# Values and half of the keys of the gated delta heads turned to tokens by 32x32 transpositions and a way through DRAM

## The reference

```python
rhs = jnp.concatenate([vc * bc[..., None], kc * (bc * jnp.exp(gam))[..., None]], axis=-1)
sol = lax.linalg.triangular_solve(lhs, rhs, left_side=True, lower=True, unit_diagonal=True)
...
k_end = kc * jnp.exp(gam[..., -1:] - gam)[..., None]
...
u = wv - jnp.einsum('bhtd,bhde->bhte', wk, S)
o = jnp.einsum('bhtd,bhde->bhte', qd, S) + jnp.einsum('bhts,bhse->bhte', qk_c, u)
S_new = ge[..., None, None] * S + jnp.einsum('bhsd,bhse->bhde', ke, u)
```

## Time and profile before

| | us |
|---|---|
| median of 3 runs | 2143.75 |
| lowest, highest | 2143.62, 2144.07 |
| the profiled execution, its own time | 2146.69 |
| its span, first to last instruction | 2145.0 |
| mean granted TensorE clock | 0.997 of full |

### The profile page before, as it was taken

How to read it: one execution, slowest core, us unless ns; L and a number is a source line. 1 busy time by engine, 2 the same in 40 slices (tenths; PEclk the granted TensorE clock), 3 DMA queues, 4 the chain that set the end, 5 groups by cost and what they waited for, 6 DMA issues and landing times.

```text
span 2145.0 us, 30741 instructions
## 1 busy us (share of the span) xinstructions
PE 2126.3 (99%) x11364; PEld 1757.1 (82%) x11364; DVE 1298.0 (61%) x1625; ACT 1109.0 (52%) x1472; POOL 165.5 (8%) x265
## 2 busy tenths in 40 slices
PE   9999999999999999999999999999999999999998
PEld 7888888888888787888878888878888788888886
DVE  6446555464544867676766564566546845566466
ACT  6554545454444848474755454445444544545443
POOL 7000000000000100101010000100001211000012
PEclk9999999999999999999999999999999999999999
DMA  9856566666565555454646755755558566555654
GB/s 338 266 182 212 174 217 191 196 199 222 179 205 177 154 163 155 145 165 134 180 145 210 259 185 177 213 151 173 187 190 293 181 210 180 177 164 179 203 176 159
DMA packets 211577, 410.98 MB, mean 192 GB/s; under 512 B 14096, under 2 KB 31009, under 8 KB 211070
## 3 DMA queue, kind: packets, MB, share of 16 engines
q1 hardware_dynamic: 199440, 369.94, 55.2%
q0 software_dynamic: 9712, 30.98, 4.7%
q10 hardware_dynamic: 2304, 8.39, 1.1%
HBM read 395.19 MB, written 14.07 MB: 191 GB/s over the span
## 4 chain that ended last, share of the span: by engine, by line
PE 90%; DVE 4%; ACT 3%; issue 3%; DMA 1%; DVEq 0%; ACTq 0%; SPq 0%
PE stream_psum L669 27%; PE stream_psum L671 26%; PE stream_psum L670 26%; PE heads_psum L639 2%; ACT w_high L1108 1%; DVE w_low L1538 1%; DVE work L1724 1%; ACT work L1108 1%; PE heads_psum L1025 1%; PE heads_psum L988 1%; PE heads_psum L969 1%; PE heads_psum L860 1%; PE heads_psum L841 1%; DMA w_raw<-in_w_mem_kv 1%; PE heads_psum L790 0%
## 5 line engine op out<-in xcount | busy, mean ns | idle before, releaser
L1538 DVE TENSOR_TENSOR w_low<-w_raw,w_high 128x1024 fp32r<-128x1024 f32 x688 | 829.8, 1224 | 624.4 <-ACT w_high L1108 622.6
L1108 ACT ACTIVATE w_high<-w_raw 128x1024 fp32r<-128x1024 f32 x688 | 711.8, 1057 | 463.7 <-PE stream_psum L671 365.3
L669 PE MATMUL stream_psum<-w_high,x_high 128*128 128x512 f32 x1856 | 739.5, 398 | 1.6 <-issue 1.6
L671 PE MATMUL stream_psum<-w_high,x_low 128*128 128x512 f32 x1856 | 723.8, 390 | 0.0
L670 PE MATMUL stream_psum<-w_low,x_high 128*128 128x512 f32 x1856 | 723.0, 390 | 0.0
L669 PEld LDWEIGHTS stream_psum<-w_high,x_high 128*128 128x128 f32 x1856 | 348.7, 188 | 74.6 <-issue 4.0
L671 PEld LDWEIGHTS stream_psum<-w_high,x_low 128*128 128x128 f32 x1856 | 348.4, 188 | 73.8
L670 PEld LDWEIGHTS stream_psum<-w_low,x_high 128*128 128x128 f32 x1856 | 348.8, 188 | 70.0 <-issue 1.9
L669 PE MATMUL stream_psum<-w_high,y_high 128*128 128x512 f32 x896 | 353.2, 394 | 2.1 <-DVE y_low L2001 2.1
L671 PE MATMUL stream_psum<-w_high,y_low 128*128 128x512 f32 x896 | 349.5, 390 | 0.0
L670 PE MATMUL stream_psum<-w_low,y_high 128*128 128x512 f32 x896 | 349.4, 390 | 0.0
(11 more groups left out here) (324 smaller groups left out, 1272.2 us busy)
## 6 DMA issues: line engine op xcount, KB each, us to landing
w_raw<-in_w_in SPq DMA_DIRECT2D x528, 512.0 KB, 4.4
w_raw<-in_w_out SPq DMA_DIRECT2D x128, 512.0 KB, 5.1
w_raw<-in_w_mem_kv SPq DMA_DIRECT2D x32, 512.0 KB, 5.8
turned_scratch<-work POOLq DMA_DIRECT2D x40, 128.0 KB, 3.5
work<-turned_scratch POOLq DMA_DIRECT2D x10, 512.0 KB, 5.6
work<-rows_scratch POOLq DMA_DIRECT2D x8, 512.0 KB, 5.1
proj<-in_mem_t SPq DMA_DIRECT2D x8, 256.0 KB, 7.1
work<-in_x_t SPq DMA_DIRECT2D x4, 512.0 KB, 7.0
```

The source lines that it names most:

```text
L669: pe.matmul(acc, hi[:, k, sl(m)], w, start=first, stop=False)
L671: return pe.matmul(acc, lo[:, k, sl(m)], w, start=False, stop=final)
L1108: return act.activation(dst, src, func, **kw)
L1538: tt(WL[:, c % RING, :], RAW[:, c % RING, :], WH[:, c % RING, :].bitcast(F32), ALU.subtract).then_inc(lo_done, 1)
```

## The change

Keys (their first 128 tokens, the only ones that the state update reads) and values no longer pass TensorE. VectorE transposes their 32x32 blocks in SBUF (`turned_k`, `turned_v`), which leaves each block inside its own 32 partitions. GpSimd stores the result in DRAM with eight DMAs, four of 128 KB (values) and four of 64 KB (keys), and loads it back with two, in an order that puts tokens on the partitions. Values then lie in four pieces of 32 features per row of partitions, and the products with them read and write through views of four pieces. VectorE scales both in SBUF (`ke`, `v`) just before `tt6`. The key products `kk` take the place in the step list where `k0t` stood; the steps of VectorE behind `nq` stand one step earlier.

```diff
@@ -90,7 +90,8 @@
     rel_d = nc.dram_tensor("rel_scratch", (A_H, COPIES, BIASW), F32, kind="Internal").ap()
-    turned_d = nc.dram_tensor("turned_scratch", (P, U), F32, kind="Internal").ap()
+    turned_d, values_d = [nc.dram_tensor(f"turned_{n}scratch", (P, U), F32, kind="Internal").ap() for n in ("", "values_")]
+    keys_d = nc.dram_tensor("turned_keys_scratch", (P, NBLK), F32, kind="Internal").ap()
     memt_d = [nc.dram_tensor(f"mem_{n}_scratch", (P, KT, S), F32, kind="Internal").ap() for n in ("high", "low")]
@@ -165,6 +166,7 @@
         turned_out, turned_in = sem("turned_stored"), sem("turned_loaded")
+        values_out, values_in = sem("turned_values_stored"), sem("turned_values_loaded")
         rows_out, rows_in, kv_in = sem("rows_stored"), sem("rows_loaded"), sem("kv_loaded")
@@ -182,7 +184,7 @@
         EIGHT = range(1, 7)
-        DN_PE = steps_of(sem("dn_pe"), ["k", "q", "v", "ssk", "k0t", "kk0", "kk1", "ssq", "vt0", "vt1", "qk0", "qk1"]
+        DN_PE = steps_of(sem("dn_pe"), ["k", "q", "v", "ssk", "kk0", "kk1", "ssq", "qk0", "qk1"]
                       + [f"{n}{l}" for l in LVS for n in ("x", "t")] + ["x6", "tt6"]
@@ -194,9 +196,9 @@
         DN_V = steps_of(sem("dn_dve"), ["g"] + conv_names(1) + conv_names(0) + ["silu1"] + conv_names(2)
-                        + ["nk", "silu0", "silu2", "ke", "at0", "at1", "at2", "at3", "at51", "at53", "at6", "nq", "v0", "v1"]
+                        + ["nk", "turned_k", "silu0", "silu2", "turned_v", "at0", "at1", "at2", "at3", "at51", "at53", "at6", "nq"]
                         + [f"row{k}" for k in EIGHT] + [f"{n}{k}" for k in EIGHT for n in ("part", "less")]
-                        + ["inv8", "tt2", "t2", "qkt0", "qkt1", "t3", "tt3", "t4", "full1", "full3", "top0", "top1", "full2", "full23", "t5", "full01", "full0", "tt6"]
+                        + ["inv8", "tt2", "t2", "qkt0", "qkt1", "t3", "tt3", "t4", "full1", "full3", "top0", "top1", "full2", "full23", "t5", "full01", "full0", "ke", "v", "tt6"]
                         + ["f1a", "r0", "r1", "r2", "r3", "f1b", "ss", "rs", "fr", "fg"])
@@ -556,6 +558,14 @@
                     if l == 4:
+                        wait_alone(pool, *done(DN_V, "turned_v", g))
+                        for a in range(4):
+                            for d, u, n in ((values_d, 11, S), (keys_d, 10, P)):
+                                pool.dma_start(bass.AP(d.tensor, a * n, [[4 * n, QUART], [QUART * 4 * n, 4], [1, n]]),
+                                               wk(u, 4 * n)[sl(a, QUART), :].rearrange("p (c r) -> p c r", c=4)).then_inc(values_out, 16)
+                        wait_alone(pool, values_out, g * 128 + 128)
+                        pool.dma_start(wk(2), values_d).then_inc(values_in, 16)
+                        pool.dma_start(wk(10, NBLK), keys_d).then_inc(values_in, 16)
                         pool.wait_ge(*done(DN_PE, "x3", g))
@@ -803,7 +813,8 @@
                 AT, TTs = wk(5).rearrange("p (s t) -> p s t", t=P), wk(7).rearrange("p (s t) -> p s t", t=P)
-                V = wk(2).rearrange("p (h m t) -> p h m t", h=4, m=M)
+                V = wk(2).rearrange("p (c h m t) -> p h m c t", c=4, h=4, m=M)
+                by_parts = lambda ap: ap.rearrange("p (c t) -> p c t", c=4)
                 KE = wk(11, 512).rearrange("p (h t) -> p h t", h=4)
@@ -826,11 +837,6 @@
                 yield from gap(6)
-                pe.wait_ge(*done(DN_V, "nk", g))
-                for h in range(4):
-                    last = tr(H[:, 2, sl(h)], CV[:, 1, h, 0:P])
-                last.then_inc(*signal(DN_PE, "k0t"))
-                yield from gap(2)

@@ -861,25 +867,16 @@

-                pe.wait_ge(*done(DN_V, "conv233", g))
+                pe.wait_ge(*done(DN_V, "nk", g))
                 products("kk", 0, 1)
-                yield
+                yield from gap(3)
                 pe.wait_ge(*done(DN_ACT, "sqq", g))
-                pe.wait_ge(*done(DN_V, "ke", g))
                 for i in range(2):
...
                 yield from gap(2)
-                pe.wait_ge(*done(DN_V, "silu2", g))
-                pe.wait_ge(*done(DN_ACT, "lnq", g))
-                for p in range(2):
-                    for h in (0, 1):
-                        for m in range(M):
-                            last = tr(H[:, 2 + p, sl(2 * h + m)], CV[:, 2, 2 * p + h, sl(m)])
-                    last.then_inc(*signal(DN_PE, f"vt{p}"))
-                yield from gap(2)
-                yield from gap(2)
-                pe.wait_ge(*done(DN_V, "v1", g))
+                yield from gap(4)
+                pe.wait_ge(*done(DN_V, "nq", g))
                 products("qk", 2, 0)
@@ -910,7 +907,7 @@
                 for h in range(4):
-                    last = pe.matmul(H[:, 0, sl(h)], TT[:, h, 0, :], V[:, h, 0, :], start=True, stop=True)
+                    last = pe.matmul(by_parts(H[:, 0, sl(h)]), TT[:, h, 0, :], V[:, h, 0], start=True, stop=True)
                 last.then_inc(*signal(DN_PE, "u0"))
@@ -929,7 +926,7 @@
                 for h in range(4):
-                    last = pe.matmul(H[:, 1, sl(h)], TT[:, h, 1, :], V[:, h, 1, :], start=True, stop=True)
+                    last = pe.matmul(by_parts(H[:, 1, sl(h)]), TT[:, h, 1, :], V[:, h, 1], start=True, stop=True)
                 last.then_inc(*signal(DN_PE, "u1"))
@@ -1735,17 +1732,21 @@
                 tt(wk(1), wk(1), wk(7), ALU.mult).then_inc(*signal(DN_V, "nk"))
+                dve.wait_ge(*done(DN_V, "nk", g))
+                dve.transpose(wk(10, NBLK).rearrange("p (c h t) -> p h c t", c=4, h=4), CV[:, 1, :, 0:P].rearrange("p h (c t) -> p h c t", c=4)).then_inc(*signal(DN_V, "turned_k"))
                 yield
...
                 stt(wk(2), wk(8), 1.0, wk(2), ALU.add, ALU.mult).then_inc(*signal(DN_V, "silu2"))
-                yield from gap(2)
-                dve.wait_ge(*done(DN_PE, "k0t", g))
-                tt(wk(11, 512).rearrange("p (s t) -> p s t", t=P), bank(2).rearrange("p (s t) -> p s t", t=P),
-                   cols(KD[:, bass.ds(g * 4, 4)], P), ALU.mult).then_inc(*signal(DN_V, "ke"))
-                yield from gap(2)
+                yield
+                dve.wait_ge(*done(DN_V, "silu2", g))
+                for i in range(2):
+                    last = dve.transpose(wk(11).rearrange("p (c i s t) -> p i s c t", c=4, i=2, s=4)[:, i],
+                                         wk(2 + i / 2, 512).rearrange("p (s c t) -> p s c t", s=4, c=4))
+                last.then_inc(*signal(DN_V, "turned_v"))
+                yield from gap(3)

@@ -1772,12 +1773,6 @@
                 yield
-                for p in range(2):
-                    dve.wait_ge(*done(DN_PE, f"vt{p}", g))
-                    tt(wk(2 + p / 2, 512).rearrange("p (s t) -> p s t", t=P), bank(2 + p).rearrange("p (s t) -> p s t", t=P),
-                       cols(HB[:, bass.ds(g * 4 + 2 * p, 2), :].rearrange("p h m -> p (h m)"), P), ALU.mult).then_inc(*signal(DN_V, f"v{p}"))
-                yield
-
                 wait_alone(dve, *done(DN_PL, "u8", g))
@@ -1841,18 +1836,25 @@
                 transposed(0)
-                yield from gap(2)
+                yield
+                dve.wait_ge(values_in, g * 32 + 32)
+                by_heads = lambda ap, n: ap.rearrange("p (c s t) -> p c s t", c=4, s=n)
+                tt(wk(11, NBLK).rearrange("p (s c t) -> p c s t", s=4, c=4), by_heads(wk(10, NBLK), 4),
+                   cols(over(KD[:, bass.ds(g * 4, 4)], 4), QUART), ALU.mult).then_inc(*signal(DN_V, "ke"))
+                tt(by_heads(wk(2), 8), by_heads(wk(2), 8),
+                   cols(over(HB[:, bass.ds(g * 4, 4), :].rearrange("p h m -> p (h m)"), 4), QUART), ALU.mult).then_inc(*signal(DN_V, "v"))
+                yield
                 dve.wait_ge(*done(DN_PE, "tt6", g))
...
                 F1 = wk(10.5, 512).rearrange("p (s t) -> p s t", t=P)
-                V = wk(2).rearrange("p (h m t) -> p h m t", h=4, m=M)
+                V = wk(2).rearrange("p (c h m t) -> p h m c t", c=4, h=4, m=M)
                 dve.wait_ge(*done(DN_PE, "qs", g))
...
                 for h in range(4):
-                    stt(V[:, h, 1, :], H[:, 2, sl(h)], NEB[:, bass.ds(g * 4 + h, 1), 1], V[:, h, 1, :], ALU.mult, ALU.add).then_inc(*signal(DN_V, f"r{h}"))
+                    stt(V[:, h, 1], H[:, 2, sl(h)].rearrange("p (c t) -> p c t", c=4), NEB[:, bass.ds(g * 4 + h, 1), 1], V[:, h, 1], ALU.mult, ALU.add).then_inc(*signal(DN_V, f"r{h}"))
                 yield from gap(2)
```

## The result

The changed kernel takes 2155.18 us (median of 5 runs, 2153.21 to 2156.44) against 2144.07 for the kernel before, run beside it: ratio 1.0044 (95% interval 1.0033 to 1.0056). That is slower by more than the 0.2% I called noise, and outside my range. The profiled execution took 2155.14 us with a span of 2153.0, 8.0 us longer than before's 2145.0.

A forecast was written before the change was run, and what follows sets the result against it. TensorE, busy in 99% of the span, was taken as the bound. Per group 1.38 us saved less waits of 0.9 and 0.45 left 0.3 to 0.5 us in all: 2143.4 us forecast, range 2140.8 to 2147.6.

The forecast's parts named there:

- GpSimd and DMA: Eight stores and two loads on GpSimd in the delta stage: hidden, priced at nothing, bounds 0 and 2 us per group.
- TensorE's saving: Twelve key and value transposes leave TensorE in each group: 1.38 us per group saved, 5.5 in all.
- First new wait: At chunk 256, `turned_k` delays the query silu, ScalarE and `w_low`: TensorE waits 0.9 us per group.
- Second new wait: At the group's end the norm comes before `w_low` of chunk 269: TensorE waits 0.45 us per group.
- Chunks 258 and 259: Behind chunk 256, with inversion steps moved up: slack of 0.2 us at 258 and 0.7 at 259, so no wait.
- `ke` and `v`: VectorE's scalings before `tt6`, 0.6 and 1.1 us: priced at nothing; uncovered they would cost 1.8 us per group.
- `ut4`: GpSimd's product that TensorE's `x4` needs: ready in time behind the ten issues, with room for 2.1 to 2.5 us.
- (c): Rival: GpSimd's issues and stores make `ut4` late for TensorE's `x4`; 3.2 us a group, 2156 us, or 2148.5; chance 0.12.
- (a): Rival: only one of the two new waits comes, giving back 1.8 to 3.6 us: 2140 to 2142 us; chance 0.15.
- (b): Rival: TensorE's full saving of 5.5 us, `w_low` of 256 on time: 2138.2 us, or 2137.0; chance 0.06.
- (d): Rival: small losses (thin slacks, update in pieces, late weight loads) of 0.5 to 1 us a group: 2145.4 to 2147.4 us; chance 0.17.

The follow-up runs named there:

- e8: The changed kernel again, unedited, for a second profile and time: 2153.78 us, ratio 1.0035 to the kernel before.
- e7: The changed kernel with its eight stores but without the two loads and VectorE's wait for them: 2146.50 us, ratio 1.0005 to the kernel before.
- after: The changed kernel as first measured and profiled, against the kernel before: 2155.18 us, ratio 1.0044.
- e1: The changed kernel without the ten DMAs and VectorE's wait for them: 2146.37 us, ratio 1.0005 to the kernel before.
- e6: The changed kernel with the order of e4 and the DMAs moved early, loads right behind `ut3`: 2141.82 us, ratio 0.9981 to the kernel before.
- e4: The changed kernel with `turned_k` behind the query silu and the norm one slot later: 2149.03 us, ratio 1.0017 to the kernel before.
- e5: The changed kernel with the order of e4 and without the ten DMAs: 2142.78 us, ratio 0.9986 to the kernel before.
- e2: The changed kernel with TensorE's 12 transposes a group put back, results unused: 2156.83 us, ratio 1.0053 to the kernel before.
- e9: The changed kernel with the early DMAs of e6 but VectorE's order unchanged: 2146.40 us, ratio 1.0009 to the kernel before.

## Why the prediction was wrong

**The step that failed** is in "GpSimd and DMA": "The added 6 MB over the stage are small against 411 MB; a weight load a microsecond later meets a ring with several microseconds to spare. Price nothing, bounds 0 and 2 us per group." I asked which data the new transfers could delay, found only weights, and compared bytes over the whole run. The stream that had no spare microseconds was TensorE's own instructions, and my own showed it: I read the start of `x4` there and not its 1.11 us. The runs price the loads at 7.3 us (e8 against e7), and 7.0 by the chunks of e8's trace, 5.3 by those of after's: 1.3 to 1.8 us a group, inside the bounds that I wrote beside the zero and then left out of the range. The Trainium skill, page "Runtime: NRT & Kernel Launch", section "Instruction fetch mechanics", says that instructions come in blocks of 16 KiB by a DMA queue of their own and that the cost is mostly hidden. On the size the trace agrees (1.36 MB in 83 packets); hidden it is not in the small products beside 768 KB of loads, where TensorE runs 64 products in 0.75 us, against some 0.23 us for one stream matmul.

**TensorE's saving**: 1.38 a group forecast, 1.3 measured (5.2 in all, not 5.5). Right in kind, a little too large. My sign for it, 5 us less busy time, failed in after (1.3 less), where TensorE also ran a stretch at the lower clock; in e1 it is 5.2 less and in e6 6.3.

**First new wait**: 0.9 forecast, 0.88 measured, 0.65 in group 3 (forecast 0.15 less there; it was 0.23). The cause was right: e4 and e5 move `turned_k` behind the query silu and the wait is gone; e2 gives TensorE its old work back and the wait is gone too. **Second new wait**: 0.45 forecast, 0.47, 0.46, 0.50 and 0.38 measured. Chunks 258 and 259 do not wait, `ke` and `v` are hidden (VectorE doesn't wait for the load), and `ut4` waited for x3 and not the other way round. What I left out is the 0.15 us that the chunk behind the second wait loses. With loads out of the way the chain as forecast remains, and e1, e7 and e9 lie 0.8, 0.9 and 1.9 us above the kernel before, where I had it 0.3 to 0.5 below. By the chunks of their traces 0.3 to 0.6 of that is in the stage (the smaller saving and the 0.15 a group); the rest is outside it and has no cause here.

**The rivals.** (c) had the right sign and the right suspect, the eight stores and two loads, but the wrong way: it went through `ut4`, which was in time, and e7 shows the stores free. That its 2156 lies near the measured time is chance. (a) and (b) fail, since both waits came. (d) named weight loads late beside the traffic. They were: from 690 to 1200 us ScalarE waits ten times and 23.7 us in all for `w_raw`, against five times and 9.3 before. But of these waits none reached TensorE. So the slower side had a chance of 0.11 from one mechanism, and the mechanism that decided was not on the list.

**What stays open.** The timed difference to before is 11.1 us in the first set and 8.2 in the second, of which the account has the loads' 7 and 0.5 to 1.9 for the rest; the first set holds some 2 us that I can't place, and its profile shows 2.0 ahead of the stage that e8's doesn't. Stops that end at the lower clock may be more frequent in the timed runs than in the profiled ones; a time alone does not show it. Why a packet of instructions starts later while loads are in flight (its place in a queue, or a DMA engine that is taken) wasn't tried, nor why it was late enough for small stops in e5, without any load. And 2.7 us of e2's median have no cause here.

## What to carry to other kernels

Before pricing a transfer at nothing, look at which stretch of the compute engine it lands in: beside big matmuls (e6, e9) 768 KB stopped TensorE nowhere, beside bursts of small ones 1.3 to 1.8 us a group, where the fetch of the engine's own instructions had no time to spare (that it is the fetch rests on the dates of the packets). An idle time with "issue" and no semaphore in the middle of equal instructions is the mark of it, and a row of equal products that is slower than its neighbours is a first sign; moving the loads 10 us earlier took all of it away. And a small operation costs by its place and not its length: 0.7 us of transposition ahead of the one operation that ScalarE waited for cost 0.9 us a group, behind it nothing.

## What the runs showed that I had not expected

- A late packet of instructions goes with a stop of TensorE of up to 2.3 us, although the queue uses 0.3% of the DMA time.
- Of GpSimd, eight DMA issues beside VectorE's work took 0.55 us each (752.45 above), while its product `ut3` stayed at the 1.72 us of the earlier trace rows.
- The granted clock fell to 1.2 GHz for some 3 us behind idle times of TensorE of 2.0 us (after, at 60 us), 2.13 (e8), 2.16 (e2, group 1) and 2.34 (e4, group 0), and stayed at 2.4 behind 1.5 (e8, at 60 us), 1.77 (after), 1.89 (e4, group 3) and 2.22 (e2, group 0). So the length of the idle time alone does not decide it. Each such fall cost 1.2 to 1.6 us on top of the idle time.
